# Two small TensorE steps inside the even mixer of a decoder step, moved to four column tiles

## What is computed

```
p = h @ w_in                       # 1024 x 4104; h = rmsnorm(x, norm_mix)
qa, fa, ia, oga, qkv, z, a, bb = split(p)      # a and bb: the last 8 columns, 4 heads each
ext  = concat([conv_buf, qkv])                 # short causal convolution over 4 rows
conv = silu(conv1d(ext, conv_w))
beta = sigmoid(bb)
g    = -exp(a_log) * softplus(a + dt_bias)
... gated delta rule with q, k, v from conv, g and beta; HGRN2 with qa, fa, ia
out: ..., ext[:, -3:]              # the last conv rows, an output for prompt and for samples
```

## Time and profile before

| what | value |
|---|---|
| median of 3 runs | 1053.67 us (1052.16 to 1054.51) |
| the profiled execution's own time | 1056.3 us |
| its span, first to last instruction | 1054.6 us |
| PE busy | 1036.6 us (98%) |
| DVE busy | 677.4 us (64%) |
| ACT busy | 512.1 us (49%) |
| POOL busy | 92.4 us (9%) |
| mean DMA rate | 169 GB/s |
| granted TensorE clock, mean | 0.997 |

### The profile page before, as it was taken

How to read it: one execution, slowest core, us unless ns; L and a number is a source line. 1 busy time by engine, 2 the same in 40 slices (tenths; PEclk the granted TensorE clock), 3 DMA queues, 4 the chain that set the end, 5 groups by cost and what they waited for, 6 DMA issues and landing times.

```text
span 1054.6 us, 21635 instructions
## 1 busy us (share of the span) xinstructions
PE 1036.6 (98%) x8498; PEld 1018.5 (97%) x8498; DVE 677.4 (64%) x888; ACT 512.1 (49%) x699; POOL 92.4 (9%) x156
## 2 busy tenths in 40 slices
PE   9999999999999999999999999999999999999998
PEld 8999999999898988999999999999999999999997
DVE  6766654578967667866664477666545986666443
ACT  6544443565683544644443365444435464444334
POOL 4800000111001210100000020000001030000001
PEclk9999999999999999999999999999999999999999
DMA  6665555889795423555555558555555446555551
GB/s 208 210 198 174 185 177 181 131 205 195 142 122 184 111 81 102 184 185 179 179 179 180 179 161 247 178 175 186 175 183 169 143 134 190 179 178 181 179 176 42
DMA packets 135543, 177.92 MB, mean 169 GB/s; under 512 B 5962, under 2 KB 120822, under 8 KB 135473
## 3 DMA queue, kind: packets, MB, share of 16 engines
q1 hardware_dynamic: 131888, 165.74, 54.3%
q0 software_dynamic: 3520, 11.38, 3.7%
q10 hardware_dynamic: 80, 0.05, 0.0%
HBM read 171.19 MB, written 6.52 MB: 169 GB/s over the span
## 4 chain that ended last, share of the span: by engine, by line
PE 58%; DVE 4%; DMA 1%; ACT 1%; issue 1%; DVEq 0%; ACTq 0%
PE ps L1634 19%; PE ps L1635 19%; PE ps L1636 18%; DVE w_lo L1131 1%; DMA raw<-in_ffn_w_up 1%; DVE PT L1093 1%; ACT w_hi L533 0%; DVE xw_lo L1152 0%; DVE x L1140 0%; DVE hn L1099 0%; DVE PT L1084 0%; PE ps L1784 0%; PE ps L1448 0%; PE ps L1663 0%; PE ps L1510 0%
## 5 line engine op out<-in xcount | busy, mean ns | idle before, releaser
L1131 DVE TENSOR_TENSOR w_lo<-raw,w_hi 128x1024 fp32r<-128x1024 f32 x311 | 380.8, 1227 | 298.1 <-ACT w_hi L533 297.5
L533 ACT CAST w_hi<-raw 128x1024 fp32r<-128x1024 f32 x311 | 324.6, 1049 | 435.6 <-PE ps L1636 408.7
L1634 PE MATMUL ps<-xw_hi,w_hi 128*128 128x264 f32 x1472 | 420.1, 285 | 1.1 <-DVE xw_lo L1152 0.5
L1635 PE MATMUL ps<-xw_lo,w_hi 128*128 128x264 f32 x1472 | 419.9, 285 | 0.0
L1636 PE MATMUL ps<-xw_hi,w_lo 128*128 128x264 f32 x1472 | 419.1, 285 | 0.0
L1634 PEld LDWEIGHTS ps<-xw_hi,w_hi 128*128 128x128 f32 x1472 | 278.0, 189 | 2.4 <-DVE xw_lo L1152 0.9
L1636 PEld LDWEIGHTS ps<-xw_hi,w_lo 128*128 128x128 f32 x1472 | 277.2, 188 | 0.0
L1635 PEld LDWEIGHTS ps<-xw_lo,w_hi 128*128 128x128 f32 x1472 | 276.9, 188 | 0.1
L1636 PE MATMUL ps<-a_hi,w_lo 128*128 (+1 forms) x704 | 200.3, 285 | 0.0
L1634 PE MATMUL ps<-a_hi,w_hi 128*128 (+1 forms) x704 | 199.9, 284 | 0.0
L1635 PE MATMUL ps<-a_lo,w_hi 128*128 (+1 forms) x704 | 199.9, 284 | 0.0
(11 more groups left out here) (362 smaller groups left out, 793.4 us busy)
## 6 DMA issues: line engine op xcount, KB each, us to landing
raw<-in_ffn_w_gate SPq DMA_DIRECT2D x88, 512.0 KB, 3.6
raw<-in_ffn_w_up SPq DMA_DIRECT2D x88, 512.0 KB, 3.6
raw<-in_ffn_w_down SPq DMA_DIRECT2D x88, 512.0 KB, 3.4
raw<-in_w_in_even SPq DMA_DIRECT2D x32, 512.0 KB, 8.5
raw<-in_w_out_even SPq DMA_DIRECT2D x8, 512.0 KB, 3.9
raw<-in_pool_w_in SPq DMA_DIRECT2D x8, 512.0 KB, 3.5
out<-SBUFS POOLq DMA_DIRECT2D x4, 512.0 KB, 3.8
PT<-in_x_prompt SPq DMA_DIRECT2D x2, 512.0 KB, 4.1
```

What stands on the lines that cost most here:

```text
L533: nc.scalar.copy(w_hi[:, w % SPL, :], raw[:, w % RAW, :]).then_inc(hi_done, 1)
L1131: nc.vector.tensor_tensor(w_lo[:, w % SPL, :], raw[:, w % RAW, :], w_hi[:, w % SPL, :].bitcast(F32), ALU.subtract).then_inc(lo_done, 1)
L1634: mm(out, wh, hi, start=first, stop=False)
L1635: mm(out, wh, lo, start=False, stop=False)
```

## The change

The gates' projection goes from eight accumulating products on 8 array columns to four column tiles: product k goes to rows 32 (k mod 4) on, each tile accumulates two products. The partial sums are scaled by `rstd` into `RN2` by DVE, and a further product with a summing matrix `fold` (now 128 rows) adds the four tiles; it stands behind slot 6 on PE, and DVE makes the gate rows behind `slots(6, 7)` in place of before it. The weights `WAB` are widened from 8 to 32 columns, zero beyond 8. The last conv rows are no longer transposed on full width: twelve products with the identity, 32 token columns each, on four column tiles, land in one bank; DVE copies 128 x 384 in place of 11 x 1536, and eight DMAs store them in place of two.

```diff
-        WAB = sb("WAB", [P, KD, 8])
+        WAB = sb("WAB", [P, KD, 32])
-        CROW = TU[:, :, :].rearrange("p i n -> p (i n)")[:, 0:CT * P]
+        CROW = TU[:, 0:3, :].rearrange("p i n -> p (i n)")
-        fold = sb("fold", [96, 32])
+        fold = sb("fold", [P, 32])
@@ VectorE
             dve.wait_ge(st("gb_mm"), 1)
+            V.tensor_tensor(RN2[:, :], ps[:, 7, 0:TOK], rstd[:, :], ALU.mult).then_inc(st("gb_parts"), 1)
+            slots(6, 7)
+            dve.wait_ge(st("gb_mm"), 2)
             dve.wait_ge(st("consts"), 2)
-            link(V.tensor_tensor(GB[:, 7, :], ps[0:8, 7, 0:TOK], rstd[0:8, :], ALU.mult))
-            V.tensor_scalar(GB[:, 0, :], GB[:, 7, :], ab8[:, 0:1], None, ALU.add).then_inc(st("gate_rows"), 1)
+            V.tensor_copy(GB[:, 7, :], ps[0:8, 7, 0:TOK])
+            V.tensor_scalar(GB[:, 0, :], ps[0:8, 7, 0:TOK], ab8[:, 0:1], None, ALU.add).then_inc(st("gate_rows"), 1)
             dve.wait_ge(st("gate_rows"), 1)
             link(V.tensor_scalar(GB[:, 2, :], GB[:, 0, :], 0.0, None, ALU.max))
-            slots(6, 7)
             link(tap(4, 1))
...
             dve.wait_ge(st("crow_T"), 1)
-            V.tensor_copy(CROW[0:11, :].rearrange("p (b n) -> p b n", n=512), ps[0:11, 4:7, :]).then_inc(st("crow"), 1)
+            V.tensor_copy(CROW, ps[:, 4, 0:384]).then_inc(st("crow"), 1)
...
-            dve.wait_ge(st("conv_rows_out"), 32)
+            dve.wait_ge(st("conv_rows_out"), 128)
@@ VectorE, constants
-            link(nc.vector.tensor_tensor(fold[:, :], ident[0:96, 0:32], ident[0:96, 32:64], ALU.add))
-            link(nc.vector.tensor_tensor(fold[:, :], fold[:, :], ident[0:96, 64:96], ALU.add))
+            link(nc.vector.tensor_tensor(fold[:, :], ident[:, 0:32], ident[:, 32:64], ALU.add))
+            link(nc.vector.tensor_tensor(fold[:, :], fold[:, :], ident[:, 64:96], ALU.add))
+            link(nc.vector.tensor_tensor(fold[:, :], fold[:, :], ident[:, 96:128], ALU.add))
@@ TensorE
             for k in range(KD):
-                ins = mm(ps[0:8, 7, 0:TOK], WAB[:, k, :], x[:, k, :], start=k == 0, stop=k == KD - 1)
+                j = 32 * (k % 4)
+                ins = mm(ps[j:j + 32, 7, 0:TOK], WAB[:, k, :], x[:, k, :], start=k < 4, stop=k > 3)
             ins.then_inc(st("gb_mm"), 1)
-            slots(6, 14)
+            slots(6, 7)
+            pe.wait_ge(st("gb_parts"), 1)
+            mm(ps[0:8, 7, 0:TOK], fold[:, 0:8], RN2[:, :], start=True, stop=True).then_inc(st("gb_mm"), 1)
+            slots(7, 14)
...
-            for c in range(CT):
-                ins = tr(ps[0:11, 4 + c // 4, c % 4 * P:(c % 4 + 1) * P], PT[:, 16 + c, PROMPT - 3:TOK], ident[:, :])
+            for r in range(3):
+                for j in range(4):
+                    ins = mm(ps[32 * j:32 * j + 32, 4, r * P:(r + 1) * P], PT[:, 16 + 3 * j + r, TOK - 32:TOK], ident[:, :],
+                             start=True, stop=True)
             ins.then_inc(st("crow_T"), 1)
@@ GpSimd
-            pool.dma_start(WAB[:, :, :], w_in[0, :, 4096:4104].rearrange("(k p) n -> p k n", p=P))\
+            link(G.memset(WAB[:, :, :], 0.0))
+            pool.dma_start(WAB[:, :, 0:8], w_in[0, :, 4096:4104].rearrange("(k p) n -> p k n", p=P))\
...
-            pool.dma_start(conv_p[0, 0], CROW[0:3, :]).then_inc(st("conv_rows_out"), 16)
-            pool.dma_start(conv_s[0, :, CONV - 2, :], CROW[3:11, :]).then_inc(st("conv_rows_out"), 16)
+            for j in range(4):
+                n = slice(384 * j, 384 * j + 384)
+                pool.dma_start(conv_p[0, 0, :, n], CROW[32 * j + 21:32 * j + 24, :]).then_inc(st("conv_rows_out"), 16)
+                pool.dma_start(conv_s[0, :, CONV - 2, n], CROW[32 * j + 24:32 * j + 32, :]).then_inc(st("conv_rows_out"), 16)
```

More of the change, by code:

```diff
@@ L686, in even_vector @@
             dve.wait_ge(st("ab_in"), 48)
-            V.tensor_tensor(WAB[:, :, :], WAB[:, :, :], par[:, 8:16].unsqueeze(2).broadcast_to([P, KD, 8]), ALU.mult)\
+            V.tensor_tensor(WAB[:, :, 0:8], WAB[:, :, 0:8], par[:, 8:16].unsqueeze(2).broadcast_to([P, KD, 8]), ALU.mult)\
                 .then_inc(st("wab"), 1)
@@ L1232, in _ @@
             dve.wait_ge(st("consts"), 1)
-            link(nc.vector.tensor_tensor(fold[:, :], ident[0:96, 0:32], ident[0:96, 32:64], ALU.add))
-            link(nc.vector.tensor_tensor(fold[:, :], fold[:, :], ident[0:96, 64:96], ALU.add))
-            f3 = fold[:, :].rearrange("p (h b) -> p h b", h=4)
+            link(nc.vector.tensor_tensor(fold[:, :], ident[:, 0:32], ident[:, 32:64], ALU.add))
+            link(nc.vector.tensor_tensor(fold[:, :], fold[:, :], ident[:, 64:96], ALU.add))
+            link(nc.vector.tensor_tensor(fold[:, :], fold[:, :], ident[:, 96:128], ALU.add))
+            f3 = fold[0:96, :].rearrange("p (h b) -> p h b", h=4)
             nc.vector.tensor_tensor(headm[:, :], f3[:, :, 0], f3[:, :, 1], ALU.add)
```

## The result

The changed kernel takes 1055.81 us (median of 8 runs, 1054.07 to 1057.17); the kernel before, run beside it, 1053.99 us (8 runs). The ratio is 1.0020, 95% interval 1.0011 to 1.0029: slower by 1.8 us, where 1.05 us of gain was forecast. The time lies inside the predicted range, just above the 1055.78 from which the prediction would call it slower, to which it gave a chance of 0.10.

What follows compares the result with a forecast made beforehand. The prediction took TensorE (PE) to bound the kernel, with fixed weight landings in this stage. PE's 2.6 us were lost to waits; 1.05 us at slot 16's clock remained, off the 1053.67 median: 1052.6 us, range 1050.9 to 1055.9.

Steps and rivals of the forecast that it cites:

- PE's part: TensorE work: 2.6 us saved at the gates' projection, 0.5 lost to the fold, 0.5 saved at conv rows; net 2.6.
- The gate rows, ACT's stand and the cast of slot 10: Gate rows reach ACT at 236.0, ACT stands 1.9 us, slot 10's cast moves to 238.5, everything behind shifts by 1.7.
- The copy and the addition: DVE's two operations making the gate rows behind the fold: each between 0.28 and 0.42 us, taken as 0.3.
- Slot 16 hangs on the second anchor: Slot 16's weights still land at 257.99, ending ACT's wait, so slot 16 starts on PE at 266.8 again.
- The slower rival: Slot 16's weights, requested 1.7 us later, land up to 1.7 later: 1.7 us slower, 1055.4 us; chance 0.18.
- With no idle stretch before slot 16, the clock has no cause to fall there: Slot 16 on PE takes 3.0 us in place of 4.48; DVE's 1.05 us stand behind it goes: gain 1.05 us.
- The rival of the falling clock: PE's 2.2 us idle before slot 12 makes the clock fall for slots 12 and 13: gain 0.15, 1053.5 us; chance 0.30.
- the small items: POOL's memset, one more addition, and six more store DMAs putting the fourth state load up to 5.4 us later: costed at nothing.

Runs made afterwards that it cites:

- late_rows_2: The kernel before with DVE's gate rows moved behind its slots(6, 7), timed once more: ratio 1.0017, median 1055.33 us.
- late_rows: The kernel before with one line moved, DVE's gate rows behind its slots(6, 7), PE's work untouched: ratio 1.0018, median 1055.64 us.
- second profile of before: The kernel before without an edit, run and profiled again as a control: ratio 1.0005, median 1054.14 us, profiled span 1051.3 us.
- late_rows_swap: The kernel before with DVE's gate rows behind slots(6, 7) and ACT casting slot 10 ahead of its gates: ratio 1.0000, median 1054.26 us.
- act_swap: The changed kernel with ACT casting slot 10 before it waits for the gate rows: ratio 1.0010, median 1055.01 us.
- rn2_first: The changed kernel with DVE making RN2 and the gate rows ahead of tap(4, 2) and slots(6, 7): ratio 1.0011, median 1055.18 us.
- rn2_first_gates: The changed kernel with RN2 ahead of tap(4, 2), gate rows early, and conv rows as before the change: ratio 1.0002, median 1053.95 us.
- late_rows_swap_2: The kernel before with late gate rows on DVE and ACT casting slot 10 ahead of the gates, timed once more: ratio 1.0006, median 1054.64 us.

## Why the prediction was wrong

- **PE's part: right.** 2.6 us saved at the gates, 0.61 for the fold (0.5 taken; the upper bound was the truth), 0.6 at the conv rows.
- **The gate rows, ACT's stand and the cast of slot 10: right, within 0.2 us for the starts of slots 10, 12 and 16 in the profile.** PE's idle time before slot 12 was 0.52 us and not 2.2, since the clock had fallen two slots earlier. The copy and the addition were 0.41 and 0.47 us, not 0.3 each, and the fold was late by nothing.
- **"Slot 16 hangs on the second anchor": the step that failed.** The landing of slot 16's weights was taken as fixed, on the argument that with a queue "full all along" "a later request lands when it did". The delay of the request was right: it comes 1.68 us later in the changed kernel (h + 21.91 and 20.23), where 1.7 was predicted. But the 20 profiles show that the landing follows: for requests 1.8 us later in the median it comes 1.0 us later, and in late_rows_2, with nothing changed but DVE's order, at h + 31.65. The profile that the prediction was made from hid this, since its load took 10.1 us from request to landing, where 9.0 is the median of the 20; so the changed kernel's weights landed where that profile's had (h + 30.24 and 30.29). The slower rival names this mechanism, and had 0.18 of the chance. That its price, 1.7 us, is near the 1.82 between the medians is partly luck: the landings moved by less than that, and the profiles of the late_rows pairs do not follow it.
- **"With no idle stretch before slot 16, the clock has no cause to fall there": right for the execution shown, wrong as the term of the sum.** The 1.05 us was the undoing of a fall that the second profile of before does not have; only about one execution in five of that kernel (29 of 147) has the low mean clock of the first, and these are 1.1 us slower in the median. Of a median the term could give back nearly nothing. It was the whole of the predicted gain. So the forecast failed twice: its gain was not there to be had, and the later landing that it put at nothing is among what was lost.
- **The rival of the falling clock:** the clock did fall, before slot 12 and not after it, and cost nothing that shows in the profile. As the explanation of the loss it has late_rows against it (the clock of before, the same loss).
- **The conv rows' part and the small items:** 1.0004 (0.9995 to 1.0013), no effect that can be told from none. Eight stores of about 0.5 us each did put POOL's fourth state load back, to 266.43, and no one waited for it.

Shown: the moved gate rows are enough for the loss (late_rows, 1.0018 and 1.0017, both intervals above 1). Supported, not settled: that ACT's queue is the way (late_rows_swap lies 1.38 and 0.69 us lower, with overlapping intervals). Open: how that order on ACT reaches the end time, since the request of slot 16 is no earlier with it; and whether DVE's own order has a part. Open as well: act_swap and rn2_first keep 0.0010 with both parts of the change, while rn2_first_gates has 1.0002. The intervals overlap, and a small cost of the conv rows' part beside the gates' part is neither shown nor excluded.

## What to carry to other kernels

Ahead of any saving on a nearly full engine, ask what its next fixed appointment hangs on: here slot 16 hung on ACT's queue and a DMA, so 2.6 us less work on TensorE bought nothing, while gate rows made later on DVE cost 1.8 us. When a step is moved behind another one on its engine, look at what stands behind its consumer in the consumer's queue; here it was a weight cast, and putting the cast first was one line, with a median 0.7 to 1.4 us lower. A term that rests on something that one execution shows (a fall of the clock, one landing) needs a second execution before it counts against a median. The same holds for a pair of traces that seems to prove a mechanism: the second pair here showed 1.0 us at the end, the first 0.4 us and the opposite order at slot 16.

## What was unexpected of the hardware

- Executions of one kernel differ in how long PE stands at the same place, and in what the clock does there: before slot 16 the kernel before stood 0.58 us in one profile and went on at 2.4 GHz, 1.50 us in the other and went on at 1.2 GHz. The runs with a mean clock of 0.997 or less are 1.1 us slower in the median (1054.68 and 1053.55, 147 runs).
- A fall of the clock can be free: behind the idle 1.83 us before slot 10, slots 10 and 11 ran at a mean clock of 0.66 for 5 us, and PE still had to wait 0.52 us for slot 12's banks.
- With twelve or more products, or 28 waits, added to PE's stream, PE's idle time at the start of the third SwiGLU, some 400 us later, is 0.80 to 1.81 us in all eight profiles and at most 0.46 in the other twelve; undoing it changed the trace and not the median.
- A load of 512 KB asked for at the same time after h (22.05 us) landed 6.4 us later in one profile and 8.6 in the other (late_rows_swap and late_rows_swap_2).
- The product with the identity on four column tiles, 0.86 us for twelve blocks, beats the twelve transposes' 1.47, although each product is two records where a transpose is one.
